# The first FFN's gate turned by VectorE in 32x32 squares that transfers inside SBUF put in place, and other turns given back to TensorE

## The reference: what is computed

```python
a = causal_dwconv(h @ w_gate[l], conv_w[l], conv_b[l])   # three taps along the tokens
y = (jax.nn.silu(a) * (h @ w_up[l])) @ w_down[l]
x = x + gt2[:, None, :] * y
```

## Time and profile before

| | |
|---|---|
| median of three executions | 2653.85 us |
| the profiled execution | 2654.21 us, span 2652.4 us |
| mean granted TensorE clock | 0.998 |
| PE busy | 2604.7 us, 98% |
| DVE busy | 1949.2 us, 73% |
| ACT busy | 1298.9 us, 49% |
| DMA engines | mean 221 GB/s |
| first FFN's loop (850 to 1424 us): DVE busy, DMA share | 458.95 of 574 us, 0.68 |

### The profile page before, as it was taken

How to read it: one execution, slowest core, us unless ns; L and a number is a source line. 1 busy time by engine, 2 the same in 40 slices (tenths; PEclk the granted TensorE clock), 3 DMA queues, 4 the chain that set the end, 5 groups by cost and what they waited for, 6 DMA issues and landing times.

```text
span 2652.4 us, 33313 instructions
## 1 busy us (share of the span) xinstructions
PE 2604.7 (98%) x11877; PEld 2149.9 (81%) x11877; DVE 1949.2 (73%) x2399; ACT 1298.9 (49%) x1577; POOL 230.4 (9%) x164
## 2 busy tenths in 40 slices
PE   4999999999999999999999999999999999999998
PEld 3888887888888888888888887887888888888887
DVE  7968777878877888888878865677566666666665
ACT  4455644455454444444444554556454444444443
POOL 0000000100000000000001210240001111111110
PEclk9999999999999999999999999999999999999999
DMA  9989768578867666666666665644666666666663
GB/s 381 402 311 338 250 200 288 187 241 282 299 224 243 223 221 223 220 224 222 222 191 180 193 180 178 190 143 132 197 185 196 194 195 192 192 196 190 193 194 119
DMA packets 280791, 585.60 MB, mean 221 GB/s; under 512 B 22032, under 2 KB 24492, under 8 KB 279796
## 3 DMA queue, kind: packets, MB, share of 16 engines
q1 hardware_dynamic: 280340, 583.61, 67.5%
q10 hardware_dynamic: 352, 0.71, 0.1%
HBM read 582.07 MB, written 2.11 MB: 220 GB/s over the span
## 4 chain that ended last, share of the span: by engine, by line
PE 93%; DVE 4%; DMA 1%; issue 1%; ACT 1%; DVEq 0%; SPq 0%; ACTq 0%
PE lin L510 29%; PE lin L512 29%; PE lin L511 29%; DVE sb_wlo L1640 1%; DMA sb_ada<-in_w_ada_dram 1%; PE aux L511 1%; PE aux L512 1%; PE aux L510 1%; PE aux L545 0%; PE aux L1000 0%; PE aux L842 0%; DMA sb_gt_bias<-in_b_ada_dram 0%; DVE sb_acc L1731 0%; DVE sb_hid_f L2119 0%; DVE sb_hidf L2119 0%
## 5 line engine op out<-in xcount | busy, mean ns | idle before, releaser
L1640 DVE TENSOR_TENSOR sb_wlo<-sb_raw,sb_whi 128x1024 fp32r<-128x1024 f32 x896 | 1114.3, 1249 | 619.1 <-ACT sb_whi L1055 613.7
L1055 ACT ACTIVATE sb_whi<-sb_raw 128x1024 fp32r<-128x1024 f32 x896 | 945.3, 1059 | 1157.2 <-PE lin L512 1080.5
L510 PE MATMUL lin<-sb_whi,sb_act_hi 128*128 128x512 f32 x2620 | 1034.8, 395 | 2.7 <-DVE sb_wlo L1640 2.2
L512 PE MATMUL lin<-sb_whi,sb_act_lo 128*128 128x512 f32 x2620 | 1021.4, 390 | 0.0
L511 PE MATMUL lin<-sb_wlo,sb_act_hi 128*128 128x512 f32 x2620 | 1020.8, 390 | 0.0
L510 PEld LDWEIGHTS lin<-sb_whi,sb_act_hi 128*128 128x128 f32 x2620 | 492.9, 188 | 107.7 <-issue 6.1
L512 PEld LDWEIGHTS lin<-sb_whi,sb_act_lo 128*128 128x128 f32 x2620 | 492.5, 188 | 103.8
L511 PEld LDWEIGHTS lin<-sb_wlo,sb_act_hi 128*128 128x128 f32 x2620 | 493.0, 188 | 100.5 <-issue 1.7
L510 PE MATMUL lin<-sb_whi,sb_hid_hi 128*128 128x512 f32 x704 | 276.0, 392 | 4.4 <-DVE sb_hid_lo L2137 4.4
L512 PE MATMUL lin<-sb_whi,sb_hid_lo 128*128 128x512 f32 x704 | 274.5, 390 | 0.0
L511 PE MATMUL lin<-sb_wlo,sb_hid_hi 128*128 128x512 f32 x704 | 274.5, 390 | 0.0
(11 more groups left out here) (370 smaller groups left out, 1887.1 us busy)
## 6 DMA issues: line engine op xcount, KB each, us to landing
sb_raw<-in_w_in_dram SPq DMA_DIRECT2D x176, 512.0 KB, 6.6
sb_raw<-in_ffn_w_gu_dram SPq DMA_DIRECT2D x176, 512.0 KB, 3.8
sb_ada_in<-in_w_ada_dram SPq DMA_DIRECT2D x128, 512.0 KB, 4.9
sb_raw<-in_gla_w_in_dram SPq DMA_DIRECT2D x96, 512.0 KB, 3.8
sb_raw<-in_w_gate_dram SPq DMA_DIRECT2D x88, 512.0 KB, 3.8
sb_raw<-in_w_up_dram SPq DMA_DIRECT2D x88, 512.0 KB, 4.4
sb_raw<-in_w_down_dram SPq DMA_DIRECT2D x88, 512.0 KB, 4.2
sb_raw<-in_ffn_w_down_dram SPq DMA_DIRECT2D x88, 512.0 KB, 3.6
```

Source lines behind the costliest of these rows:

```text
L510: pe.matmul(o, h, whi[:, w], start=first and q == 0, stop=False)
L512: m = pe.matmul(o, l, whi[:, w], start=False, stop=last and q == 1)
L1055: act.activation(whi[:, idx % RING * HALF:(idx % RING + 1) * HALF], raw[:, idx // 2 % RING, idx % 2 * HALF:(idx % 2 + 1) * HALF], ACT.Copy ...
L1640: dve.tensor_tensor(wlo[:, c], raw[:, idx // 2 % RING, idx % 2 * HALF:(idx % 2 + 1) * HALF], whi[:, c].bitcast(fp32), ALU.subtract).then_i ...
```

## The change

Three parts.

1. In the loop of the first FFN the gate is turned without PE. DVE transposes `gbuf` in 32x32 squares within each quadrant of 32 partitions, on all 128 lanes, in four instructions (`turn_gate` on DVE, index 12) into `gate_sq`. SP, behind the third up slab and its piece of w_ada, issues 16 transfers inside SBUF of 32 partitions by 1 KB (`exchange_gate`), which put quadrant a's squares q into quadrant q of `gate_ex`. ACT copies them to `gpad` in four instructions at index 16 (`exchanged_pad`) in place of two at 13. Chunks 0 and 10 are turned by PE as before.
2. At the ends: in F1e chunk 9's `ubuf` is turned by PE (behind half 1) and not by DVE, with `hid_high` and `hidden` at 5 in place of 7. In F2e chunk 10's is turned by PE (behind half 17, once `up_mul` has come), with `hid_high` and `hidden` at 21 in place of 22, reading PSUM. The second FFN's `hidden` is two instructions in place of one.
3. In C1 PE scores pair p behind half 3p + 2 in place of 3p + 3; relu and `add_heads` move from 3p + 7 to 3p + 6, the mask from 28 to 27.

```diff
+    gate_sq = at("gate_sq", [P, 4, 2 * S // 2], ARENA + 49 * KB)
+    gate_ex = at("gate_ex", [P, 4, 2 * S // 2], ARENA + 53 * KB)
...
+            def exchange_gate(j):          # SP
+                sp.wait_ge(sem("gate_T"), j + 1)
+                sp.wait_ge(sem("gpad_made"), j)
+                for a in range(4):
+                    for q in range(4):
+                        sp.dma_start(gate_ex[32 * q:32 * q + 32, a, :], gate_sq[32 * a:32 * a + 32, q, :]).then_inc(sem("gate_in"), 16)
...
-                gate_up(it, name, 24, 8, it + 1, w_u, u0)
+                gate_up(it, name, 24, 8, it + 1, w_u, u0, exchange_gate if n == 0 else None)
...
-            if idx % 3 == 0 and 1 <= p <= NIX // 2:      # PE, C1
-                ix_scores(p - 1, p - 1)
-            if idx % 3 == 0 and p < NIX // 2:
+            if p < NIX // 2 and step == 0:
                 ix_turn(p, p)
+            if p < NIX // 2 and step == 2:
+                ix_scores(p, p)
...
-                run = hooks(it + 1, 9, 1)               # PE, FFN loop
+                run = hooks(it + 1, -1, 1)
...
+                if idx == 1 and n == 0:                  # PE, F1e and F2e
+                    turn_up(FB - 2)
-                if idx == 17 and n == 0:
+                if idx == 17:
                     turn_up(FB - 1)
...
+            def exchanged_pad(j):          # ACT
+                act.wait_ge(sem("gate_in"), 256 * j)
+                for f in range(4):
+                    m = act.activation(gpad[:, f, 2:].rearrange("p (t a b) -> p t a b", t=TB, a=4),
+                                       gate_ex[:].rearrange("p a (f t b) -> p f t a b", f=4, t=TB)[:, f], ACT.Copy)
+                m.then_inc(sem("gpad_made"), 1)
...
-                    add(13, lambda: gate_pad(j))
+                    add(16 if phase == name else 13, lambda: (exchanged_pad if phase == name else gate_pad)(j))
...
-            add(HID_AT, lambda: hid_high(FB - 2))
-            add(HID_AT + 15 if n else 21, lambda: hid_high(FB - 1, hid2_hi, hid2_f))
+            add(HID_AT if n else 5, lambda: hid_high(FB - 2))
+            add(21, lambda: hid_high(FB - 1, hid2_hi))
...
+            def turn_gate(j):              # DVE
+                g = G0[name + "p"] + 6 * j - 1
+                dve.wait_ge(free0, g)
+                dve.wait_ge(free1, g)
+                if j > 1:
+                    dve.wait_ge(sem("gate_in"), 256 * (j - 1))
+                for q in range(4):
+                    m = dve.transpose(gate_sq[:, q, :].rearrange("p (f t b) -> p f t b", f=4, t=TB),
+                                      gbuf[:].rearrange("p t (f q d) -> p f q t d", f=4, q=4)[:, :, q])
+                m.then_inc(sem("gate_T"), 1)
...
+                if n == 0 and phase == name:
+                    add(12, lambda: turn_gate(j))
...
-            for q, parts in enumerate(TURNS):            # DVE, F1e and F2e
+            for q, parts in enumerate(TURNS if n else ()):
                 add(4 + q, lambda parts=parts: turn_up(FB - 2, parts))
-                if n:
-                    add(19 + q, lambda parts=parts: turn_up(FB - 1, parts, hid2_f))
-            add(HID_AT, lambda: hidden(FB - 2))
-            add(HID_AT + 15 if n else 21, lambda: hidden(FB - 1, hid2_hi, hid2_lo, hid2_f))
+            add(HID_AT if n else 5, lambda: hidden(FB - 2, by_tensor=n == 0))
+            add(21, lambda: hidden(FB - 1, hid2_hi, hid2_lo, True))
```

## The result

| | median of the runs | lowest to highest | profiled execution | span | granted clock |
|---|---|---|---|---|---|
| before | 2653.86 us (4 runs) | 2653.71 to 2656.31 | 2654.21 us | 2652.4 us | 0.998 |
| after | 2686.69 us (4 runs) | 2685.34 to 2688.14 | 2685.34 us | 2683.6 us | 0.992 |

The change makes the kernel slower by 1.2%: ratio 1.0118, 95% interval 1.0105 to 1.0131. The forecast was 2645.7 (2637 to 2657). It was rival 2 that came, and beyond the price that the prediction gave it (2656.5 to 2667).

What follows compares the result with a forecast made beforehand. The prediction took TensorE (PE) to bound the kernel: 8.0 + 2.3 + 5.4 = 15.7 us less, 7.2 us given back to waits for the exchanged gate, so 2654.21 - 8.5 = 2645.7 us, range 2637 to 2657.

Steps and rivals of the forecast that it cites:

- rival 2: First loop, free bank at half 16: late exchange costs more than all gains, 2656.5 to 2667 us; chance 0.18.
- What bounds the kernel: Whole kernel: PE, busy 98% of the span and 93% of the chain; only its instructions or waits change time.
- PE's saving in the loop: First FFN's loop: nine passes lose their eight PE transposes, 0.89 us each pass, 8.0 us less.
- DVE's transposes at no cost: First loop: four transposes on DVE, 0.44 us each, 1.75 us a pass; 1.6 us are left, so costed at nothing.
- Rival 4: First loop: 128-lane transposes cost four times 436 ns, some 6 us a pass, 54 in all, 2692 us; chance 0.04.
- The transfers: First loop, SP: sixteen issues at 0.42 us, landing 2.3 later; PE waits 0.8 us a pass, 7.2 in nine.
- What may be late, T + 11.9: First loop, T the end of half 9 (922.02): the gate may land until 33.9 before PE waits at half 16.
- The two ends: First FFN's end 2.3 us less, second's 5.4 us less, as PE's waits for gbuf and hid_lo there go.
- C1 and C2 at nothing: Indexer in C1 and the 0.6 us wait in C2: counted together as nothing, +0.7 to -0.7 us.
- The slower side: Whole kernel: chance 0.14 of a slower result, from the far part of rival 2 and Rival 4.

Runs made afterwards that it cites:

- the fastest kernel: The changed kernel with ACT's copies of the exchanged gate at 18 instead of 16, convolution at 20 and 22, sigmoid and its product at 24: 2639.61 us, ratio 0.9943.
- the DRAM kernel: The changed kernel, but from the second pass on the 16 transfers bring the same shape from DRAM instead of gate_sq: 2654.27 us, one run.

## Why the prediction was wrong

- **What bounds the kernel; PE's saving in the loop.** Right. 8.0 us fewer, and the fastest kernel shows passes of 65.3 us.
- **DVE's transposes at no cost.** Right (alone they leave the time where it was, 2648.1 beside 2647.9), and below the price: 0.40 us each and not 0.44 (1.4 us a pass), with all 128 lanes in less time than 32 took in the earlier trace rows. Rival 4 is gone.
- **The transfers: the step that failed.** "The two ends are 0.36 and 0.475; I take 0.42": it was 0.66 in the second pass, 0.63 from one ordinary issue to the next. Start T + 3.7 (4.1 forecast), fifteen pitches 10.0 (6.3), last issue to landing 1.8 (2.3): landing at T + 15.5 where T + 12.7 stood. What may be late, T + 11.9, held: 15.5 - 11.9 = 3.6, measured 3.56. The rows were loads from DRAM. The chip runs the same shape from DRAM at a median pitch of 0.46, and from SBUF at 0.63 to 0.64 whatever the bytes and partitions. The trace before had a transfer inside SBUF too, of 64 partitions (SP's queue in the timeline of the kernel before):

```profile
219.25 0.55 SPq L387 DMA_DIRECT2D sb_k_ixT<-sb_k_ixT  x1
```

  It was the nearest row by kind, and it was passed over for rows that were nearer by count and by number of partitions. With it (0.55, and the gap of 0.04) the prediction's own formula gives 4.1 + 8.8 + 2.3 = T + 15.2, a wait of 3.3 a pass, 30 us: the measured 29.8. That it comes so close is in part luck: the pitch is still short, by some 1.1 us in fifteen, and start and landing were forecast 0.4 and 0.5 too late.
- **The clock: a term that was missing.** The prediction took the low clock out at the second FFN's end, from the earlier trace rows, and did not ask whether a new wait would bring it into the loop. Eight of nine waits did: 15.2 us, 1.7 a pass, half as much again as the waits. Rival 2's worst case, 2667, had the sum of the waits right (29 us), by luck: its pitch of 0.475 was too short by 2.9 us in fifteen and its 3.9 from issue to landing too long by 2.1. It lacked the clock; with it, it reads 2682.
- **The two ends.** Right: -2.1 for -2.3, -5.3 for -5.4, no wait moved elsewhere.
- **C1 and C2 at nothing.** Right within the bounds given (0 to -0.5 over that stretch, in one execution of each kernel).
- **The chances.** The slower side had 0.14. The range's end rested on the nearer half of rival 2, whose condition was a pitch of 0.475 at most; the one row of the same kind, 0.55 long, lay beyond it.

The cause of the slowdown is settled: undone, moved or shortened, it goes as the wait does. Why an issue inside SBUF takes SP longer was not settled, only on what it doesn't depend. Two ways to make the gate land earlier were not tried: one transfer for a whole quadrant's four squares, and issuing the exchange first. In the pass shown the squares were ready at 928.66, and SP's first transfer of them began at 930.78, behind a half and the piece of w_ada.

## What to carry to other kernels

A series of small transfers is paid by the issue: take its price from a row with the same two memories, multiply it by the count, and put the consumer behind that, not at the first index where it may stand. An instruction hooked early costs nothing while it is on time, and holds every drain behind it once it is late; list all of them, on every engine of the queue. To each wait that a forecast admits on TensorE, add what its clock may cost after it.

## What was not expected of the hardware

- A median issue on SP's queue, and the median pitch: 0.59 and 0.63 us from SBUF to SBUF, 0.42 and 0.46 for the same shape from DRAM, 0.43 and 0.475 in the earlier trace rows; 0.59 and 0.63 with a quarter of the bytes, 0.60 and 0.64 over 128 partitions. In most passes one issue, the third or fourth of the series, takes 0.9 to 1.2 us.
- From the issue of 32 KB to its landing 1.8 to 4.3 us, median 2.3: the first transfer of a series takes 3.4 to 4.3, the last 1.8 in all nine passes. The Trainium skill, "DMA: Bandwidth & Descriptors", "Anatomy of one DMA", has 2.0 us fixed for DMAs that GpSimd issues; these are SP's, the low end lies a little below it, and the spread is wide.
- A stream transpose of 128 lanes x 256 took 0.40 us, and 0.44 from 32 lanes to 32 others.
- PE's clock after a wait: in the kernel after, slow starts (0.43 apart, 6 to 14 of them) behind eight waits of 2.4 to 3.66 us, and none behind that of the seventh pass, with 3.67 the longest. None either behind the DRAM kernel's waits of 3.3 and 2.2, behind the first of the kernel with a quarter of the columns (3.15), nor behind any of 1.0 to 1.6. The length of the wait alone doesn't decide, and the run of slow starts at 161 us has no wait before it.
